# Gate and up of the first layer's experts by seven products of quarters, and a new order of work in the second's

## The chip, the cores and the metric

The kernel runs on one core of a Trainium2 chip. Its time is the device time of one execution in microseconds; lower is better. The engines are TensorE (PE, with its weight loads as PEld), VectorE (DVE), ScalarE (ACT), GpSimd (POOL), and the SyncE queue (SP), which issues most DMAs.

## The reference, cut to what matters

A trunk of two layers over 1024 rows and 256 context rows of 1024 float32 numbers: modulation, a mixer, and then 16 experts. In the first layer the contexts go through the experts too, in the second they don't. What changes lies in the experts:

```python
def expert_choice_ffn(h, w_router, w_gate, w_up, w_down):
    cap = CAPACITY_FACTOR * n // N_EXPERTS            # 128 rows, 32 contexts per expert
    aff = softmax(h @ w_router); gate, idx = top_k(aff.T, cap)
    xg = h[idx]                                       # gathered per expert
    hid = silu(xg @ w_gate) * (xg @ w_up)             # 1024 x 1024 weights for each expert
    out = (hid @ w_down) * gate
    return zeros_like(h).at[idx].add(out)
```

## The kernel before

All matrices are float32; each float32 matmul is two instructions on TensorE. The program is a row of stages (`project`, attention, `mix_out`, `experts`, `front`, `scan`, ...). In a stage each engine has its own instruction stream in program order, tied to the others by semaphores only. Weights for a following stage can be loaded ahead into buffers of classes named `...Ahead` (`FrontAhead` for the stage `front`, `DownAhead` for the first layer's down weights).

**First layer, `experts`** (L2357 on). Per expert, GpSimd gathers 128 rows (`xg`) and 32 contexts (`xc`) by indirect DMA. TensorE transposes them (`turn_rows`, L2711 and L2714), ScalarE and VectorE scale and shift them into `xT` with 160 columns (128 rows, 32 contexts). For each of 8 blocks of 128 hidden columns TensorE multiplies gate and up weights as the standing operand by `xT` (L2756, 8 matmuls each), ScalarE takes silu, VectorE the product; so the hidden values come out already transposed. Down is two halves of 8 matmuls with 512 columns (`down_rows`, L2722), between them the contexts as four strips of 32 output partitions at once (`down_ctx`, L2731). GpSimd adds the results into `moe` by indirect DMA. The stage begins with eight steps each of two thirds of a modulation (`opening`, L244) and ends with eight of another (`closing`). The SP queue's order at the start is: vectors, modulation weights, gate and up of expert 0, the stored first third (`store_third`, which waits until it is in memory), down of expert 0 after the first transposes, `following.load` (some 25 loads, L2313), gate and up of expert 1, the second stored third, 4 MB `load_columns`, down of expert 1, then a loop.

**Second layer, `last_experts`** (L2786 on), no contexts. Gate and up are each made by seven products of quarters in place of eight (the Strassen-Winograd scheme). A quarter product has 4 x 2 matmuls: 64 rows' halves of `xT` (or sums of them, `sx`) stand, 256 columns of weights or of sums of weights stream, and two column halves of the array work at once on the two halves j. VectorE makes the sums of weight quarters (`weight_sum`, four per matrix, 128x2048 numbers each, L3017 to L3026) and of row quarters (`row_sums`). Products share four PSUM banks X, Z, W, V. ScalarE copies four of them out (`keep`), VectorE adds the rest to them (`quarter`) and multiplies (`hidden`). TensorE then transposes the hidden values (`turn_hidden`, L3123), ScalarE copies them to `hT`, and down takes 32 instructions (L3167) into banks W and V, alternating between the two. ScalarE takes the left half of y from W (L2986), VectorE the right half from V. The order of one expert on TensorE:

```python
for i in (GATE, UP):
    for p in PRODUCTS:              # (5, 1, 2, 6, 3, 7, 4)
        multiply(e, i, p)
turn_hidden(e, 0)
turn_rows(e + 1)
turn_hidden(e, 1)
```

Product 2 of gate waits for `ya` (ScalarE has taken the left half of y), product 4 for `yv`. In the last expert the final sums begin: the SP queue first issues `following.load_rows` (8 loads of the rows of `res` into the gate weights' place), then, once the scatter of expert 14 is in memory, the loads of `moe` into `m` (`load_sum`). ScalarE squares them (`square`) between two `keep`, VectorE gates (`gated`, L3063) and sums them (`summed`, L3068).

In `scan`, SP stores eight tiles in order and issues `following.load_qk` for the band attention after the sixth.

## Time and profile before

| | |
|---|---|
| median of 3 runs | 3416.34 us (3415.37 to 3417.86) |
| the profiled execution: time, span | 3414.7 us, 3413.0 us |
| TensorE busy | 3160.0 us, 93% of the span |
| VectorE, ScalarE, GpSimd busy | 46%, 30%, 15% |
| mean granted TensorE clock | 0.962 |
| read from and written to memory | 585.65 MB, 90.97 MB, 198 GB/s |

The profile is of one execution. Busy shares are means over stages with different limits, so each part has to be read in its own window. "Idle before" in square brackets is the time an engine stood before an instruction, with what ended it; times are from the start of the span.

### The profile page before, as it was taken

The numbers are of one execution on the slowest core, as the hardware profiler recorded it, in microseconds if no ns is written. First come the engines' busy times: TensorE is split into PE (matmuls) and PEld (weight loads), VectorE is DVE, ScalarE is ACT, GpSimd is POOL, SyncE is SP. The second block draws the span as 40 slices with busy tenths as digits, with TensorE's granted clock in tenths as the row PEclk, the third lists the DMA queues.
The fourth block names the chain that finished last, engine by engine and source line by source line (L and its number), as shares of the span: only waits on it lengthen the run. The fifth ranks groups of instructions, "written<-read, shape, count | busy, mean of one in ns | idle before, by whom it ended". The sixth has DMA issues, their size and how long they took to land. (4 is left out here: it accounts for less than half of the span.)

```text
span 3413.0 us, 52595 instructions
## 1 busy us (share of the span) xinstructions
PE 3160.0 (93%) x19496; PEld 2216.1 (65%) x19496; DVE 1559.8 (46%) x3170; ACT 1009.8 (30%) x2323; POOL 525.1 (15%) x639
## 2 busy tenths in 40 slices
PE   6999989999987999999999799899899299999996
PEld 4888856667435788787887565666664155555553
DVE  3212178778654010101101254566785666666565
ACT  4111156755330111101111152235554222222222
POOL 0010235110100101011110120254101101111112
PEclk9999999999987999999999899999999599999998
DMA  6336353053639977787777630100414589999996
GB/s 231 130 108 114 92 188 113 20 132 95 241 132 339 352 267 250 244 275 245 265 255 262 232 121 1 56 22 28 112 33 173 197 293 334 326 335 339 338 335 257
DMA packets 340390, 672.38 MB, mean 197 GB/s; under 512 B 84041, under 2 KB 133065, under 8 KB 334017
## 3 DMA queue, kind: packets, MB, share of 16 engines
q1 hardware_dynamic: 308384, 568.00, 47.9%
q0 software_dynamic: 13616, 47.32, 5.5%
q10 hardware_dynamic: 18240, 55.16, 4.3%
q8 instruction: 83, 1.36, 0.2%
q14 instruction: 67, 0.54, 0.1%
HBM read 585.65 MB, written 90.97 MB: 198 GB/s over the span
## 5 line engine op out<-in xcount | busy, mean ns | idle before, releaser
L2756 PE MATMUL experts_gu_ps<-experts_xT,experts_wg 128*128 128x160 f32 x2048 | 301.3, 300 | 2.6 <-DVE experts_xT L2630 2.6
L2756 PE MATMUL experts_gu_ps<-experts_xT,experts_wu 128*128 128x160 f32 x2048 | 299.4, 299 | 0.0
L2756 PEld LDWEIGHTS experts_gu_ps<-experts_xT,experts_wg 128*128 128x128 f32 x2048 | 287.9, 191 | 9.9 <-issue 9.9
L2756 PEld LDWEIGHTS experts_gu_ps<-experts_xT,experts_wu 128*128 128x128 f32 x2048 | 285.6, 190 | 0.0
L2653 DVE TENSOR_TENSOR experts_hid<-experts_sil,experts_gu_ps 128x160 f32<-128x160 f32 x128 | 41.1, 321 | 516.1 <-ACT experts_sil L2584 516.1
L2722 PE MATMUL experts_y_ps<-down_ahead_wd,experts_hid 128*128 128x512 f32 x512 | 228.3, 599 | 0.0
L2584 ACT ACTIVATE experts_sil<-experts_gu_ps 128x160 f32<-128x160 f32 x128 | 38.9, 304 | 604.9 <-PE experts_gu_ps L2756 604.9
L2722 PEld LDWEIGHTS experts_y_ps<-down_ahead_wd,experts_hid 128*128 128x128 f32 x512 | 94.6, 190 | 114.4 <-issue 113.7
L3458 PE MATMUL front_pb_ps<-kept_hT,front_ahead_w 128*128 128x512 f32 (+1 forms) x384 | 138.7, 521 | 0.7 <-DVE kept_dt L3509 0.7
L3167 PE MATMUL experts_w_ps<-experts_wd,experts_hT 128*128 128x512 f32 x256 | 130.8, 597 | 8.5 <-issue 7.8
L3167 PE MATMUL experts_v_ps<-experts_wd,experts_hT 128*128 128x512 f32 x256 | 129.6, 592 | 0.0
L2671 DVE TENSOR_SCALAR experts_y<-experts_y_ps,experts_wt 128x512 f32<-128x512 f32 x16 | 12.0, 751 | 249.0 <-PE experts_y_ps L2722 249.0
L554 PE MATMUL proj_x_ps<-first_w,first_shared 128*128 128x256 f32 x480 | 115.0, 383 | 3.1 <-DMA first_w<-in_l_w_in 3.1
L3912 PE MATMUL scan_f_ps<-scan_w,kept_hT 128*128 128x512 f32 x256 | 116.4, 597 | 0.0
L3458 PEld LDWEIGHTS front_pb_ps<-kept_hT,front_ahead_w 128*128 128x128 f32 x384 | 72.4, 190 | 62.7 <-issue 59.4
L2524 POOL DMA_INDIRECT moe<-experts_yc,experts_ixsc x16 | 25.8, 1610 | 522.5 <-ACT experts_yc L2601 522.5
L2953 ACT ACTIVATE experts_kept<-experts_x_ps 128x256 f32<-128x256 f32 x96 | 36.8, 384 | 231.7 <-PE experts_x_ps L3159 230.4
L554 PEld LDWEIGHTS proj_x_ps<-first_w,first_shared 128*128 128x128 f32 x480 | 91.7, 192 | 15.9 <-DMA first_w<-in_l_w_in 3.4
L635 DVE TENSOR_TENSOR proj_ob<-proj_z_ps,proj_kept 128x256 f32<-128x256 f32 x30 | 12.7, 424 | 190.3 <-PE proj_z_ps L554 189.5
L867 ACT ACTIVATE attn_a_e<-attn_a_e,attn_a_nmx 128x1280 f32<-128x1280 f32 (+1 forms) x80 | 96.6, 1209 | 8.0 <-DVE attn_a_e L929 8.0
L3167 PEld LDWEIGHTS experts_w_ps<-experts_wd,experts_hT 128*128 128x128 f32 x256 | 47.3, 190 | 65.5 <-issue 64.5
L3167 PEld LDWEIGHTS experts_v_ps<-experts_wd,experts_hT 128*128 128x128 f32 x256 | 48.6, 190 | 61.2 <-issue 61.2
(561 smaller groups left out, 6308.7 us busy)
## 6 DMA issues: line engine op xcount, KB each, us to landing
experts_wg<-in_l_w_gate SPq DMA_DIRECT2D x64, 2048.0 KB, 8.5
experts_wu<-in_l_w_up SPq DMA_DIRECT2D x64, 2048.0 KB, 12.7
down_ahead_wd<-in_l_w_down SPq DMA_DIRECT2D x32, 2048.0 KB, 10.6
experts_wd<-in_l_w_down SPq DMA_DIRECT2D x32, 2048.0 KB, 7.7
down_ahead_wd<-in_l_w_mod SPq DMA_DIRECT2D x16, 1024.0 KB, 9.2
proj<-proj_ob ACTq DMA_DIRECT2D x60, 256.0 KB, 2.3
first_w<-in_l_w_in SPq DMA_DIRECT2D x6, 2048.0 KB, 10.1
attn_a_mod_w<-in_l_w_mod ACTq DMA_DIRECT2D x12, 1024.0 KB, 6.5
```

The source lines that it names most:

```text
L554: mm = nc.tensor.matmul(to[:, left], by[k], at[k], start=(k == 0 and n in (0, 1, 5)), stop=(k == HALF - 1 and n in (3, 5, 6)), skip_group_ ...
L635: nc.vector.tensor_tensor(ob[:, slot, 0, right], Z[:, left], kept[:, 2], ALU.add).then_inc(dve_out, 1)
L867: nc.scalar.activation(e[:, s, m, 0:w], e[:, s, m, 0:w], ACT.Exp, bias=nmx[:, s, m:m + 1], scale=-1.0, accum_out=sums[:, s, m:m + 1]).then ...
L2524: pool.indirect_dma_start(moe.rearrange("t (j c) -> (t j) c", j=4), bass.IndirectOffsetOnAxis(ap=ixsc[:, 0:1], axis=0), yc[:], None, compu ...
L2584: nc.scalar.activation(sil[:, f % 2, :], GU[f % 2][:, 0, 0:N], ACT.Silu).then_inc(sil_done, 1)
L2653: nc.vector.tensor_tensor(hid[:, f, :], sil[:, f % 2, :], GU[f % 2][:, 1, 0:N], ALU.mult).then_inc(hid_done, 1)
L2722: mm = nc.tensor.matmul(Y[h][:], hid[:, k, 0:CAPX], wd[:, h, k, :], start=(k == 0), stop=(k == KD - 1))
L2756: mm = nc.tensor.matmul(GU[f % 2][:, part, 0:N], w[:, h, k, c * P:(c + 1) * P], xT[:, k, :], start=(k == 0), stop=(k == KD - 1))
L2953: nc.scalar.activation(kept[:, KEPT.index(p), :], bank[:, 0:COLS], ACT.Copy).then_inc(act_out, 1)
L3167: return nc.tensor.matmul(Y[h][:], hT[:, k, :], w[DOWN][:, k, h * BANK:(h + 1) * BANK], start=(k == 0), stop=(k == KD - 1))
L3458: mm = nc.tensor.matmul(pb[n % 4][:, 0:width], w[:, s, k, at:at + P], hT[:, k, first:first + width], start=(k == 0), stop=(k == KD - 1))
L3912: mm = nc.tensor.matmul(F[:], kept.hT[:, k, t * P:(t + 1) * P], w[:, int(kind == "q"), k, :], start=(k == 0), stop=(k == KD - 1))
```

## The change

`experts` is replaced by `first_experts`, which does gate and up of the 128 rows by the same seven products. Contexts are now gathered as 128 rows of 256 numbers (four strips of one context each) and are multiplied on their own, for gate and for up, in four strips of 32 output partitions (`multiply_ctx`); hidden rows and hidden contexts are transposed afterwards. The sums of weight quarters lie in `following.w`, the weight buffer of `front`, so `load_columns` moves behind the last expert. The gathers run one expert further ahead. In both layers the order of products becomes (5, 1, 2, 4, 6, 3, 7), products 5 and 1 of the next expert's gate go before the down product, the next rows are transposed after product 4 of up, both halves of the gate (and up) weights are loaded after product 7, and the weight sums are made in a new order. In the tail `load_rows` goes behind the first four `load_sum`, and two tiles are gated in advance, not four. In `scan`, `load_qk` goes one store earlier. Three semaphores of `Choice` become one, and two small buffers of the modulation are lent by others.

```diff
-PRODUCTS = (5, 1, 2, 6, 3, 7, 4)
+PRODUCTS = (5, 1, 2, 4, 6, 3, 7)
+def first_experts(nc, name, K, listed, normed, mod, g_pre, w_gate, w_up, w_down, moe, following, down, last_third):
...
+        sums = [following.w[:, i].rearrange("p k n -> p (k n)").rearrange("p (s k j n) -> p s k j n", s=2, k=HALF, j=2) for i in (GATE, UP)]
...
+            def _(sp):
...
+                for n in range(opening.slots, opening.steps):
+                    opening.load(sp, n)
+                for i in (GATE, UP):
+                    for half in range(2):
+                        load(i, half, 0)
+                opening.store_third(sp, 0)
+                sp.wait_ge(opening.multiplied, START + opening.steps)
+                load_down(0)
+                following.load(sp)
+                opening.store_third(sp, 1)
+                with sp.Fori(0, E - 1) as e:
+                    for i in (GATE, UP):
+                        sp.wait_ge(mm_done, multiplied(e, i, 7))
+                        for half in range(2):
+                            load(i, half, e + 1)
+                    sp.wait_ge(y_done, right_at(e))
+                    load_down(e + 1)
+                for i in (GATE, UP):
+                    sp.wait_ge(mm_done, multiplied(E - 1, i, 7))
+                    for n in range(4):
+                        closing.load(sp, 4 * i + n)
+                following.load_columns(sp)
...
+            def _(dve):
...
+                def gates_and_up(e, last=False):
+                    weight_sum(e, UP, 7)
+                    hidden_ctx(e)
+                    after(dve, ht_done, e * 3)
+                    for q in range(4):
+                        quarter(e, GATE, q)
+                    weight_sum(e, UP, 4)
+                    for q in range(4):
+                        if q == 1 and not last:
+                            weight_sum(e + 1, GATE, 5)
+                            ctx_rows(e + 1)
+                        if q >= 2:
+                            dve.wait_ge(hid_done, hidden_at(e, q - 1))
+                        quarter(e, UP, q)
+                        hidden(e, q)
+                        if q == 1 and not last:
+                            row_sums(e + 1, True)
+
+                def rest_of_sums(e):
+                    weight_sum(e, GATE, 6)
+                    row_sums(e, False)
+                    weight_sum(e, GATE, 4)
+                    weight_sum(e, UP, 5)
+                    weight_sum(e, UP, 6)
+                    weight_sum(e, GATE, 7)
...
+                def turn_hidden(e, c):
+
+                    pe.wait_ge(hid_done, hidden_at(e, 2 * c + 2))
+                    pe.wait_ge(hid_out, copied_at(e, 2 * c))
+                    for h in range(2):
+                        for i in range(2):
+                            mm = nc.tensor.transpose(HT[:, 2 * h + i, :], gate[:, c, h, i * P:(i + 1) * P], K.ident[:])
+                    mm.then_inc(ht_done, 1)
...
+                def multiply_ctx(e, i):
+                    if i == GATE:
+                        pe.wait_ge(sx_done, ctx_rows_at(e))
+                        after(pe, hid_done, (e - 1) * 5 + 1)
+                    for half in range(2):
+                        pe.wait_ge(w_in[i][half], START + e * 16 + 16)
+                    for k in range(KD):
+                        for j in range(4):
+                            mm = nc.tensor.matmul(C[j * CAPC:(j + 1) * CAPC, i, :], xcT[:, k, :], w[i][:, k, j * CW:(j + 1) * CW],
+                                                  start=(k == 0), stop=(k == KD - 1))
+                    mm.then_inc(mm_done, 1)
...
+                def from_context_to_rows(e, following_rows):
+                    multiply_ctx(e, UP)
+                    for p in PRODUCTS[2:]:
+                        multiply(e, GATE, p)
+                    turn_hidden_ctx(e)
+                    for p in PRODUCTS:
+                        multiply(e, UP, p)
+                        if p == 4 and following_rows:
+                            turn_rows(e + 1)
+                    if following_rows:
+                        pe.wait_ge(sx_done, ctx_rows_at(e + 1))
+                    turn_hidden(e, 0)
...
+                with pe.Fori(0, E - 1) as e:
+                    from_context_to_rows(e, True)
+                    multiply(e + 1, GATE, PRODUCTS[0])
+                    turn_hidden(e, 1)
+                    multiply(e + 1, GATE, PRODUCTS[1])
+                    multiply_ctx(e + 1, GATE)
+                    pe.wait_ge(xa, START + e * 2 + 4)
+                    down_all(e)
...
 def last_experts(nc, name, K, listed, normed, mod, g_pre, w_gate, w_up, w_down, moe, following, out):
...
-                sp.wait_ge(mm_done, multiplied(E - 1, GATE, 4))
-                following.load_rows(sp, x)
                 sp.wait_ge(s_done, (E - 1) * 16)
...
+                sp.wait_ge(mm_done, multiplied(E - 1, GATE, 7))
+                following.load_rows(sp, x)
...
                 with pe.Fori(0, E - 1) as e:
-                    for i in (GATE, UP):
-                        for p in PRODUCTS:
-                            multiply(e, i, p)
+                    for p in PRODUCTS[2:]:
+                        multiply(e, GATE, p)
+                    for p in PRODUCTS:
+                        multiply(e, UP, p)
+                        if p == 4:
+                            turn_rows(e + 1)
                     turn_hidden(e, 0)
-                    turn_rows(e + 1)
+                    multiply(e + 1, GATE, PRODUCTS[0])
                     turn_hidden(e, 1)
+                    multiply(e + 1, GATE, PRODUCTS[1])
...
-                    if j == NTX - 3:
+                    if j == NTX - 4:
```

## Rows read from the trace of the kernel before

**Rows 1.** Windows, first layer's experts: window, length, busy and count by engine, PEclk, DMA, GB/s.

```profile
1230.00:1500.00 270.00, 270.00 (x1841) 221.10 (x1840) 27.23 (x75) 31.92 (x75) 30.99 (x50) 1.00 0.76 257
```

**Rows 2.** Timeline of TensorE, one expert, first layer: start, length, engine, line, operation.

```profile
1226.20 7.13 PE L2722 MATMUL experts_y_ps<-down_ahead_wd,experts_hid 128*128 128x512 f32 x16
...
1233.17 2.34 PE L2756 MATMUL experts_gu_ps<-experts_xT,experts_wg 128*128 128x160 f32 x16
...
1267.95 1.04 PE L2711 MATMUL experts_tp_ps<-ident,experts_xg 128*128 128x128 f32 x8
...
1269.52 7.13 PE L2722 MATMUL experts_y_ps<-down_ahead_wd,experts_hid 128*128 128x512 f32 x16
...
1276.59 3.66 PE L2731 MATMUL experts_yc_ps<-down_ahead_wd,experts_hid 128*32 128x256 f32 x64
...
1280.18 4.99 PE L2722 MATMUL experts_y_ps<-down_ahead_wd,experts_hid 128*128 128x512 f32 x11
```

**Rows 3.** Timeline of TensorE, one expert, second layer.

```profile
2770.86 1.95 PE L3159 MATMUL experts_z_ps<-experts_tg,experts_sx 128*64 128x256 f32 x16
...
2793.36 1.90 PE L3159 MATMUL experts_v_ps<-experts_tu,experts_xT 128*64 128x256 f32 x16
...
2795.18 0.66 PE L3123 MATMUL experts_ht_ps<-ident,experts_hid 128*128 128x128 f32 x4
...
2796.55 0.60 PE L3123 MATMUL experts_ht_ps<-ident,experts_hid 128*128 128x128 f32 x4
...
2797.67 1.10 PE L3167 MATMUL experts_w_ps<-experts_wd,experts_hT 128*128 128x512 f32 x2 [0.52 <-issue]
...
2811.57 1.95 PE L3159 MATMUL experts_z_ps<-experts_tg,experts_sx 128*64 128x256 f32 x16
```

**Rows 4.** Timeline of ScalarE and VectorE, the same expert of the second layer.

```profile
2793.57 0.38 ACT L2953 ACTIVATE experts_kept<-experts_x_ps 128x256 f32<-128x256 f32 x1 [2.99 <-PE experts_x_ps L3159]
...
2794.45 0.42 DVE L3040 TENSOR_TENSOR experts_hid<-experts_hid,experts_gate 128x256 f32<-128x256 f32 x1
...
2800.63 2.29 DVE L3022 TENSOR_TENSOR experts_wg<-experts_wg 128x2048 f32<-128x2048 f32 x1
...
2811.74 0.69 ACT L2986 ACTIVATE experts_y<-experts_w_ps,experts_wt 128x512 f32<-128x512 f32 x1 [11.09 <-PE experts_v_ps L3167]
```

**Rows 5.** Start of the first layer's experts (timeline); last row: DMA issues, 1150 to 1850.

```profile
1068.69 4.60 PE L2756 MATMUL experts_gu_ps<-experts_xT,experts_wg 128*128 128x160 f32 x16 [2.63 <-DVE experts_xT L2630]
...
1103.06 0.96 SPq L2330 DMA_DIRECT2D front_ahead_cw<-in_l_conv_b  x1
...
1114.23 6.11 SPq L257 DMA_DIRECT2D mod<-experts_opening_rows  x4
...
experts_wg<-in_l_w_gate SPq DMA_DIRECT2D x26, 2048.0 KB, 8.5
```

**Rows 6.** Timeline of the tail: last expert of the second layer and final sums.

```profile
3352.09 0.32 POOL L2920 COPY experts_ixs<-experts_index 128x1 int32<-128x1 int32 x1 [7.79 <-DMA moe<-experts_y,experts_ixs]
...
3353.19 4.91 SPq L2354 DMA_DIRECT2D experts_wg<-res  x8
...
3358.15 23.44 SPq L2884 DMA_DIRECT2D experts_m<-moe  x5
...
3370.40 1.06 ACT L2958 ACTIVATE experts_sq<-experts_m 128x1024 f32<-128x1024 f32 x1 [13.36 <-DMA experts_m<-moe]
...
3373.23 3.68 PE L3159 MATMUL experts_x_ps<-experts_wu,experts_sx 128*64 128x256 f32 x16 [11.45 <-ACT experts_kept L2953]
...
3386.32 1.23 DVE L3063 TENSOR_TENSOR experts_m<-experts_m,finish_ahead_gate 128x1024 f32<-128x1024 f32 x1 [1.49 <-ACT experts_sq L2958]
...
3397.63 1.28 DVE L3068 SCALAR_TENSOR_TENSOR experts_wg<-experts_m,experts_ms,experts_wg 128x1024 f32<-128x1024 f32 x1
```

**Rows 7.** Timeline where the scan stage ends and the band stage begins.

```profile
2396.46 3.71 DVE L3840 SCALAR_TENSOR_TENSOR band_ahead_o<-scan_total,scan_ms,scan_gn 128x256 f32<-128x256 f32 x4
...
2405.38 1.97 PE L1612 MATMUL attn_band_tr_ps<-ident,band_ahead_q 128*128 128x128 f32 x8 [9.56 <-DMA band_ahead_q<-proj]
```

More of the change, by code:

```diff
@@ L2870, in _ @@
                         sp.wait_ge(mm_done, multiplied(e, i, 7))
[L2871 to L2873 removed]
+                        for half in range(2):
+                            load(i, half, e + 1)
                     for half in range(2):
@@ L3985, in trunk @@
                 if with_ctx:
-                    experts(nc, f"experts{n}", K, listed, normed, mods[n], layer["g_pre_ffn"], *weights, moe, following, down, rest[3])
+                    first_experts(nc, f"experts{n}", K, listed, normed, mods[n], layer["g_pre_ffn"], *weights, moe, following, down, rest[3])
                 else:
```

894 lines of the change are left out of this document (464 added, 430 removed).

## The prediction

> **What bounds the kernel now.** I read the page's table of engines first, then the windows of the two expert stages, then TensorE's timeline for one expert of each layer, then what ScalarE, VectorE and the SP queue do beside it, and last the two places where TensorE stands still. In the first layer's experts TensorE is busy for the whole window, at a granted clock of 1.00, while the DMA engines are at 0.76 and VectorE has 27 us of work in 270 [rows 1]. So there the time is TensorE's instruction stream, and nothing else. One expert is 53.98 us from down product to down product: 16 blocks of gate and up (34.78), the transposes of the next rows (1.57), the down products (7.07 and 6.97) and the contexts' down product (3.59) [rows 2]. In the second layer one expert takes 40.71 us: fourteen products of 1.73 (24.23 up to the transposes), transposes of 0.50, 0.87 and 0.50, a stand of about 0.6 until hT is copied, 13.90 for down [rows 3].
>
> **Change part by part, first layer, steady state.** Removed per expert: 34.78 + 1.57 = 36.35. Added: 14 products x 1.73 = 24.2 (the same shape, 16 instructions 128*64 by 256 [rows 3]); the contexts' gate and up as strips, 64 instructions 128*32 by 256 each, the very shape of the contexts' down product, 2 x 3.59 = 7.2 [rows 2]; ten transposes for the next rows (8 rows, 2 contexts) at 0.114 (12 take 1.37 from 2795.18 to 2796.55 [rows 3]) = 1.1; eight of the hidden rows and two of the hidden contexts = 1.2. Sum 33.7.
>
> A new wait: `turn_hidden(e, 1)` needs the last hidden quarter, and product 7 is now the last. After that product's issue ends (2793.36), ScalarE's copy ends 0.6 later, VectorE's sum and product 1.5 later [rows 3, 4]; two more operations of 0.42 make it 2.45, and 0.1 for the semaphore. TensorE arrives at 0.09 + 0.50 + 1.73 = 2.3: a stand of 0.25.
>
> Now VectorE, which had no weight sums there. It gets eight of 2.29 [rows 4], some 18 us, with all else about 28 of 51.6: enough, if nothing it queues behind is late. The gate weights of the next expert are asked for after product 7 of gate. With the end of the previous down product as zero this is 3.6 + 5 x 1.73 + 0.35 = 12.6; 8.5 to landing [rows 5] gives 21.1; the sum for product 5 ends at 23.4, two context operations at 24.3. The up quarter behind them can start at 24.4 anyway, the first hidden transposes come at 25.9, VectorE is ready at 25.3. The margin is 0.6 us. I take 0.2 for both a small lateness and the seams. The up weights (asked at 26.0) are wanted by VectorE from 33.5, where it waits, but TensorE wants them at 51.6; down has 33 us. Gathers run an expert ahead, under all this. The saving is 36.35 - 33.7 - 0.25 - 0.2 = 2.2 per expert, 35 over 16; the last expert also drops the useless transposes (1.1) and waits 0.75 for hT: 0.3 more.
>
> The strips are where a page speaks against this. Row: 64 context instructions take 3.59 us [rows 2], 56 ns each, where a lone 256-column one would take half of the 512-column 0.43 us (16 in 7.07 [rows 2]); four strips thus overlap 3.8 times. The Trainium skill (TensorE: Matmul & The Clock Gate, Measured speedup vs the span model) has 3.07 times for four tiles by rows, and like values for columns. With that the two new context products would cost some 4.5 each, 1.8 more per expert; the row is this very shape, so I go by it.
>
> **First layer, first expert.** This is the largest loss I see. The SP queue issues the loads for the following stage (`following.load`) and the second stored third before its loop; the gate weights of expert 1 come after. Before, the last of `following.load` ends at 1104.02 [rows 5], and expert 0 still ran until about 1122: hidden. Now the stores of the opening third, with their wait for landing, stand ahead of the gate load too. Four took 6.11 with the queue full [rows 5]; with it empty between 2 and 8 with landing, I take 4.5. So the load goes at 1108.5, half lands at 1117.0, sum, context operations, quarter and hidden bring the first hidden transposes to 1121.3. TensorE would be there, starting 0.6 later than at 1068.69 (all eight xT blocks are on ScalarE), with 2.3 for the low clock as in the first block before (4.60 for 2.34 [rows 2, 5]), at 1069.3 + 5.8 + 7.2 + 8.6 + 0.2 + 12.1 + 1.1 = 1104.3. It stands 17.0 us, and then the clock costs another 2.3. Cover: none, VectorE's order puts that sum before the up quarters. Loss 17.0 + 2.3 + 0.6 = 19.9. The 4 MB of columns for the next stage move behind the last expert, since the sums lie in their buffer; they may slow the last scatter by 0 to 2, I take 0.5. First layer: 35.3 - 19.9 - 0.5 = 14.9 gained.
>
> **Second layer.** Products 5 and 1 of the next expert move ahead of down and cover the stand of 0.6 [rows 3]. But product 2 now follows down directly, and it writes the bank W from which ScalarE still takes the left half of y. Both halves end together there, ScalarE starts at 2811.74 and ends at 2812.43 [rows 4]; with 0.15 for the semaphore product 2 starts at 2812.6 and not at 2811.57: 1.0 lost. In the first layer the contexts' up product lies between. Per expert: -0.6 + 0.25 + 1.0 = 0.6 longer, 15 times 9.0. The first expert has all seven sums ahead of its gate quarters: VectorE needs six more of 2.29 and three row sums before the first quarter, 15.9 us, TensorE is there at about 14.8; with the seam 1.3 lost.
>
> The tail. Before, the rows of res (8 loads) go ahead of the sums m; the scatter had landed at 3352.09, m arrives at 3370.40, ScalarE waits for it with `keep` behind it, and TensorE stands 11.45 and then runs a product in 3.68 [rows 6]. Now m goes first, at the scatter's landing, and the stand is gone. What ends last then is the rows: the same bytes, asked for 1 us earlier. m and rows take 18.8 us from 3353.19 by the old rate (17.2 to the ninth load, and three more), so the rows are in 30.6 after the down product of expert 14 (3340.8: 2811.57 [rows 3] and 13 periods; the landing is 11.2 behind it, the first issue 11.8). From there VectorE has eight sums of 1.28 and six gatings of 1.23 [rows 6], 17.6, and 0.5 of waits: 48.7. Before, the last sum ended at 3398.9 [rows 6], 58.1 behind. The gain is 9.4. Second layer: 9.4 - 9.0 - 1.3 = 0.9 lost.
>
> **Scan.** q and k of the band stage are loaded after the fifth stored tile, not the sixth. Two tiles are 3.71 of VectorE, and TensorE waits 9.56 for q [rows 7]: between 0 and 1.9, I take 1.5, as other engines enter the stage about then. Other edits (one semaphore for three in `Choice`, halves of xT) cost nothing: TensorE's stream does not change with them.
>
> **Sum.** 14.9 - 0.9 + 1.5 = 15.5 off the profiled execution's 3414.7 (span 3413.0), 3399.2; the median of the runs is 1.6 above the profiled one. I predict 3400. That is 0.5%; under 0.2% (6.8 us) this kernel can't be told from no change.
>
> **Rivals.**
> 1. *Gate weights late in every expert* (slower). The margin in the first layer is 0.6 us, in the second 0.9. Each us beyond costs 15 or 16. All the gain is eaten when the half lands 10.1 us after its issue, not 8.5. For it: the load now starts as the down weights' 4 MB end, with a scatter and two gathers in flight. The Trainium skill (DMA: Bandwidth & Descriptors, Queues, rings and completion order) says that an engine takes turns between queues packet by packet, so a gather slows the load. Against it: 8.5 was measured with gathers around, and the engines are idle for a quarter of the time [rows 1]. At 2 us late past the margin in both layers the time is 3400 + 16 x 2 + 15 x 2 = 3462, at 1 late in both 3431. Chance 0.11 of more than that 1.5 in all.
> 2. *No stand in the first expert*: the small loads go out faster, or the half lands before 1104. Against: the SP row. Time 3400 - 19 = 3381. Chance 0.08.
> 3. *The wait for W costs less or the tail gives more* (the rows land sooner, TensorE's second layer hides the copy): 3388. Chance 0.14.
> 4. *No measurable change*: the stand is longer (8 us of stores) and the strips or sums lose 0.3 per expert: 3410 to 3422. Chance 0.12.
> 5. *Strips of gate and up overlap worse than those of down*: three at once instead of 3.8, 64 x 0.215 / 3 = 4.6 for 3.59 [rows 2], 2 x 1.0 x 16 = 32 more, 3432. Against: the same shape, measured. Chance 0.01. The page on tiles named above would have it so.
> The forecast itself: 0.54, its own range 3392 to 3408.
>
> Faster by over 0.2%: 0.76, within: 0.12, slower: 0.12. The range, leaving out rivals 5, the far part of 1 and the lower part of 2, is 3380 to 3418.
>
> **What would show it.** Period of the first layer 51.6 to 51.9, and of the second 41.2 to 41.4, with TensorE waiting about 1.0 before `experts_w_ps` for ScalarE's y; one stand of 15 to 19 us before the first `experts_ht_ps` near 1105; a gate load issued near 1108; no wait of ScalarE for m, and VectorE waiting for the rows in the tail. Wrong if the weight sum for product 5 waits for its DMA past 23 us in each expert, or if the strips take more than 3.7.

## The result and the profile after

The changed kernel takes 3440.4 us (median of four runs, 3435.5 to 3442.5) against 3416.7 us for the kernel before, measured beside it. The ratio is 1.0068, 95% interval 1.0054 to 1.0082: slower by 0.7%, where I had forecast 0.5% faster. The profiled execution is the fastest of the four: 3435.5 us, span 3433.7 us, 20.7 more than before.

Three anchors on TensorE split these 20.7 us: the first product of the first layer's experts, the first transposes of `front`, and the transposes of the second layer's `Choice`.

| stretch | before | after | difference | forecast |
|---|---|---|---|---|
| first layer's experts, to `front`'s first transposes | 891.0 | 898.7 | +7.7 | -14.9 |
| `front` and scan, to the second layer's `Choice` | 753.2 | 752.4 | -0.8 | -1.5 |
| from there to the end | 700.1 | 713.9 | +13.8 | +0.9 |
| mean period, first layer / second layer | 53.98 / 40.71 | 53.58 / 41.81 | -0.4 / +1.1 | -2.2 / +0.6 |

One expert of the first layer on TensorE, in the changed kernel's timeline (start, length, engine, line, operation; in brackets the idle time before it and what ended it), against [rows 2]:

```profile
1226.83 0.63 PE L2805 MATMUL experts_ht_ps<-ident,experts_gate 128*128 128x128 f32 x4 [1.08 <-DVE experts_xcT L2669]
1227.38 1.95 PE L2848 MATMUL experts_z_ps<-front_ahead_w,experts_sx 128*64 128x256 f32 x16
1229.26 0.66 PE L2805 MATMUL experts_ht_ps<-ident,experts_gate 128*128 128x128 f32 x4
1229.85 1.95 PE L2848 MATMUL experts_x_ps<-experts_wg,experts_xT 128*64 128x256 f32 x16
1231.73 3.66 PE L2860 MATMUL experts_c_ps<-experts_wg,experts_xcT 128*32 128x256 f32 x64
1235.32 4.99 PE L2868 MATMUL experts_w_ps<-down_ahead_wd,experts_hT 128*128 128x512 f32 x11
...
1275.86 1.90 PE L2848 MATMUL experts_z_ps<-experts_wu,experts_sx 128*64 128x256 f32 x16
1277.58 1.90 PE L2848 MATMUL experts_x_ps<-experts_wu,experts_sx 128*64 128x256 f32 x16
1280.50 0.63 PE L2805 MATMUL experts_ht_ps<-ident,experts_gate 128*128 128x128 f32 x4 [1.02 <-DVE experts_xcT L2669]
```

The strips are as forecast: `experts_c_ps` takes 3.59 (1231.73 to 1235.32). But TensorE stands about 1 us in each expert for VectorE (0.76 to 1.12 in the fourteen experts behind the first, 0.94 in the mean). VectorE's timeline and the SP queue's show why:

```profile
1218.13 0.42 DVE L2716 TENSOR_TENSOR experts_gate<-experts_gate,experts_up 128x256 f32<-128x256 f32 x1
1222.84 2.29 DVE L2690 TENSOR_TENSOR front_ahead_w<-experts_wg 128x2048 f32<-128x2048 f32 x1 [4.29 <-DMA experts_wg<-in_l_w_gate]
1225.05 0.42 DVE L2668 TENSOR_TENSOR experts_xcT<-experts_ht_ps,experts_gain 128x256 f32<-128x256 f32 x1
1225.51 0.43 DVE L2669 TENSOR_TENSOR experts_xcT<-experts_xcT,experts_shift 128x256 f32<-128x256 f32 x1
1225.85 0.42 DVE L2710 TENSOR_TENSOR experts_up<-experts_z_ps,experts_kept 128x256 f32<-128x256 f32 x1
1226.30 0.42 DVE L2716 TENSOR_TENSOR experts_gate<-experts_gate,experts_up 128x256 f32<-128x256 f32 x1
```

```profile
1199.41 1.00 SPq L2507 DMA_DIRECT2D down_ahead_wd<-in_l_w_down  x2
1211.94 0.93 SPq L2501 DMA_DIRECT2D experts_wg<-in_l_w_gate  x2
1225.79 0.92 SPq L2501 DMA_DIRECT2D experts_wu<-in_l_w_up  x2
```

The gate weights are asked for at 1211.94 and the sum for product 5 can start only at 1222.84: 10.9 us, not 8.5. The sum, two context operations, a quarter and a hidden product follow, and then the transposes. The windows of the same expert (length, busy and count of PE, PEld, DVE, ACT, POOL, then clock, DMA share, GB/s):

```profile
1199.30:1211.90 12.60, 12.60 (x147) 7.84 (x146) 4.13 (x5) 0.80 (x3) 5.64 (x6) 1.00 0.90 278
1211.90:1222.80 10.90, 10.90 (x100) 7.24 (x100) 3.90 (x5) 4.23 (x11) 0.67 (x4) 1.00 1.03 402
1222.80:1238.50 15.70, 14.62 (x140) 8.14 (x137) 13.46 (x16) 3.76 (x12) 0.00 (x0) 1.00 0.97 373
1238.50:1253.00 14.50, 14.50 (x90) 6.38 (x88) 4.49 (x2) 2.65 (x4) 1.62 (x1) 1.00 0.08 10
```

The mean DMA share over this expert (some 0.7) hides two halves: 39 us with the engines full, 14.5 us with nothing to move. The gate load falls into the full part.

The first expert, at the place of [rows 5] (TensorE, then SP):

```profile
1102.61 1.90 PE L2848 MATMUL experts_x_ps<-experts_wu,experts_sx 128*64 128x256 f32 x16
1117.65 1.08 PE L2805 MATMUL experts_ht_ps<-ident,experts_gate 128*128 128x128 f32 x4 [13.14 <-DVE experts_xcT L2669]
1118.66 3.16 PE L2848 MATMUL experts_z_ps<-front_ahead_w,experts_sx 128*64 128x256 f32 x16
1121.76 0.66 PE L2805 MATMUL experts_ht_ps<-ident,experts_gate 128*128 128x128 f32 x4
```

```profile
1101.92 0.59 SPq L2330 DMA_DIRECT2D front_ahead_cw<-in_l_conv_b  x1
1102.55 1.33 SPq L257 DMA_DIRECT2D mod<-experts_y  x4
1105.39 1.03 SPq L2501 DMA_DIRECT2D experts_wg<-in_l_w_gate  x2
```

The stand is there, for the reason given, at 13.1 instead of 17.0: the stores took 2.8 us with their wait, not 4.5, and the small loads ended 1.5 earlier. Behind this stand the granted clock is 0.50 (1.2 GHz) in the transposes and 0.59 in product 5: the two take 4.1 us from start to start (1117.65 to 1121.76), where they take 2.4 two experts later (1226.83 to 1229.26).

Second layer, against [rows 3]: the stand for y is there too, and the period is 41.81 (2825.02 to 2866.83).

```profile
2825.02 1.95 PE L3313 MATMUL experts_w_ps<-experts_wg,experts_xT 128*64 128x256 f32 x16 [0.84 <-ACT experts_y L3134]
...
2866.83 1.95 PE L3313 MATMUL experts_w_ps<-experts_wg,experts_xT 128*64 128x256 f32 x16 [0.84 <-ACT experts_y L3134]
```

The tail, against [rows 6]: SP asks for `m` first, ScalarE waits only 1.2 us for it, and VectorE then waits for the rows of `res`.

```profile
3379.40 1.77 SPq L3019 DMA_DIRECT2D experts_m<-moe  x4
3381.21 5.31 SPq L2354 DMA_DIRECT2D experts_wg<-res  x8
```

```profile
3400.97 2.48 DVE L3225 SCALAR_TENSOR_TENSOR experts_wg<-experts_m,experts_ms,experts_wg 128x1024 f32<-128x1024 f32 x2 [9.14 <-DMA experts_wg<-res]
```

The seam between scan and the band stage, against [rows 7]: first VectorE's last tile before the change, then SP, VectorE and TensorE in the changed kernel.

```profile
2402.41 0.88 DVE L3840 SCALAR_TENSOR_TENSOR band_ahead_o<-scan_total,scan_ms,scan_gn 128x256 f32<-128x256 f32 x2 [0.76 <-DMA mixed<-band_ahead_o]
```

```profile
2403.85 1.11 SPq L1194 DMA_DIRECT2D band_ahead_q<-proj  x2
2406.12 7.19 SPq L3841 DMA_DIRECT2D mixed<-band_ahead_o  x3
```

```profile
2412.08 0.88 DVE L4001 SCALAR_TENSOR_TENSOR band_ahead_o<-scan_total,scan_ms,scan_gn 128x256 f32<-128x256 f32 x2 [5.38 <-DMA mixed<-band_ahead_o]
```

```profile
2413.76 1.94 PE L1612 MATMUL attn_band_tr_ps<-ident,band_ahead_q 128*128 128x128 f32 x8 [12.88 <-PEq L3817]
```

The sixth tile's store now stands behind the loads of q and k, and VectorE waits 5.38 us for its buffer before the last tile, not 0.76. TensorE no longer waits for q but for the end of the stage, and longer: 12.88 us, not 9.56.

### The profile page after: what moved, and what is told of

It reads as the page before. It is cut to its first block and busy times, and to the rows that moved or that the text cites. A ratio compares the mean times of both kernels' runs of the same rounds, so it can differ in the third digit from the quotient of the medians.

```text
span 3433.7 us, 57319 instructions
## 1 busy us (share of the span) xinstructions
PE 3144.1 (92%) x21080; PEld 1975.6 (58%) x21080; DVE 1888.4 (55%) x3373; ACT 1086.4 (32%) x2510; POOL 554.7 (16%) x641
## 5 line engine op out<-in xcount | busy, mean ns | idle before, releaser
L2868 PE MATMUL experts_w_ps<-down_ahead_wd,experts_hT 128*128 128x512 f32 x256 | 114.1, 599 | 0.7 <-ACT experts_hT L2633 0.7
L2868 PE MATMUL experts_v_ps<-down_ahead_wd,experts_hT 128*128 128x512 f32 x256 | 114.1, 599 | 0.0
L2606 ACT ACTIVATE experts_kept<-experts_x_ps 128x256 f32<-128x256 f32 x96 | 36.8, 383 | 202.5 <-PE experts_x_ps L2848 202.5
L3054 POOL DMA_INDIRECT moe<-experts_y,experts_ixs x15 | 24.1, 1609 | 464.0 <-DVE experts_y L3240 464.0
L3091 ACT ACTIVATE experts_kept<-experts_x_ps 128x256 f32<-128x256 f32 x96 | 36.8, 383 | 179.8 <-PE experts_x_ps L3313 176.8
L929 DVE TENSOR_SCALAR_CACHE_REDUCE attn_a_e<-attn_a_s_ps,attn_a_nmx 128x256 f32<-128x256 f32 (+1 forms) x128 | 72.8, 613 | 27.3 <-PE attn_a_s_ps L1004 27.2
L1029 PE MATMUL attn_a_o_ps<-attn_a_v,attn_a_aT 128*128 128x128 f32 x672 | 83.1, 277 | 3.9 <-ACT attn_a_sq L882 3.9
L2777 DVE TENSOR_SCALAR experts_y<-experts_v_ps,experts_wt 128x512 f32<-128x512 f32 x15 | 11.3, 752 | 137.0 <-PE experts_v_ps L2868 137.0
L2598 ACT ACTIVATE experts_xT<-experts_tp_ps,experts_shift,experts_gain 128x128 f32<-128x128 f32 x128 | 47.9, 459 | 120.6 <-PE experts_ht_ps L2796 120.6
L1029 PEld LDWEIGHTS attn_a_o_ps<-attn_a_v,attn_a_aT 128*128 128x128 f32 x672 | 78.3, 192 | 11.4 <-issue 7.7
L3083 ACT ACTIVATE experts_xT<-experts_tp_ps,experts_shift,experts_gain 128x128 f32<-128x128 f32 x128 | 47.9, 460 | 110.0 <-PE experts_tp_ps L3268 110.0
```

The costliest lines, as they stand in the source:

```text
L929: nc.vector.tensor_scalar(e[:, s, m, c:c + w], S[i % 2][m][:, 0:w], -1.0, nmx[:, s, m:m + 1] if j else None, ALU.mult, ALU.min, accum_out= ...
L1029: mm = nc.tensor.matmul(O[:, 0:P], aT[:, kt, :], v[:, h % 2, kt, :], start=(kt * P == keys(t)[0]), stop=(kt == last))
L2598: a = nc.scalar.activation(xT[:, k, :], TP[k // 4][:, k % 4, :], ACT.Identity, bias=shift[:, 0, k:k + 1], scale=gain[:, 0, k:k + 1])
L2606: nc.scalar.activation(kept[:, KEPT.index(p), :], bank[:, 0:COLS], ACT.Copy).then_inc(act_out, 1)
L2868: mm = nc.tensor.matmul(Y[h][:], hT[:, k, :], wd[:, h, k, :], start=(k == 0), stop=(k == KD - 1))
L3083: a = nc.scalar.activation(xT[:, k, :], TP[k // 4][:, k % 4, :], ACT.Identity, bias=shift[:, k:k + 1], scale=gain[:, k:k + 1])
```

## The experiments

All ratios are to the kernel before, measured beside each kernel, with intervals of 0.0010 to 0.0014 to each side. "First layer" and "rest" are the first and third stretch of the table above, read in each kernel's one trace; a period stands for one expert near 1280 or 2900. Stretches with the same code differ by up to 2.3 us from trace to trace (first layer of the changed kernel and of e4: 898.7 and 896.4), so a difference of 2 us between two rows says nothing.

| kernel | ratio | first layer | period | rest | period |
|---|---|---|---|---|---|
| before | 1 | 891.0 | 53.98 | 700.1 | 40.71 |
| changed | 1.0068 | 898.7 | 53.7 | 713.9 | 41.81 |
| e1_columns_later | 1.0052 | 893.3 | 53.4 | 713.9 | |
| e2_sum_later | 1.0090 | 905.8 | 54.06 | 713.6 | |
| e3_stagger | 1.0060 | 898.5 | 53.55 | 713.9 | |
| e4_six_first | 1.0024 | 896.4 | | 701.3 | 40.91 |
| e5_ctx_first | 1.0027 | 886.4 | 52.64 | 714.8 | |
| e6_gather_early | 1.0041 | 886.8 | 52.61 | 714.5 | |
| e7_down_early | 1.0032 | 886.5 | 52.61 | 713.4 | |
| e8_mended | 0.9940 | 871.9 | 52.61 | 696.8 | 40.91 |
| e9_also_gather | 0.9930 | 872.1 | | 696.1 | 40.91 |
| e10_joined | 0.9926 | 871.9 | | 692.9 | 40.71 |
| e11_split_rows | 0.9950 | 871.5 | | 701.3 | 41.21 |
| e12_old_second | 0.9945 | 872.1 | | 698.5 | 40.71 |

**e1_columns_later.** The first gate and up loads of expert 1 go ahead of the stores and of `following.load`.

```diff
                 load_down(0)
+                for i in (GATE, UP):
+                    sp.wait_ge(mm_done, multiplied(0, i, 7))
+                    for half in range(2):
+                        load(i, half, 1)
+                    if i == GATE:
+                        opening.store_third(sp, 1)
                 following.load(sp)
-                opening.store_third(sp, 1)
-                with sp.Fori(0, E - 1) as e:
+                sp.wait_ge(y_done, right_at(0))
+                load_down(1)
+                with sp.Fori(1, E - 1) as e:
```

> The changed kernel, with one thing moved: in the first layer the SP queue issues the first gate and up loads of expert 1 ahead of the opening third's stores and of the 26 small loads for the next stage. Theory (the SP queue held the gate load back in the first expert alone): the gate load goes at 1090 to 1092 instead of 1105.4, the stand of 13.1 us before the first hidden transposes goes with it, and with it the low clock behind it (1.4 to 2.3): 14 to 16 us less than the changed kernel, ratio to the kernel before about 1.002, periods unchanged at 53.7 and 41.8. Rival (the small loads only move and hold back the down or up loads of expert 1, or the weights land late anyway as 6 MB are then in flight): a stand of 5 us or more stays in the first two experts, less than 8 us gained.

The first stand went: the first down product starts at 1111.7 instead of 1127.8. But the small loads now kept the SP queue until 1140.6, past the end of expert 0, and the down and gate loads of the next expert came at 1140.7 and 1142.5. A second stand takes half of it back:

```profile
1153.97 1.90 PE L2855 MATMUL experts_x_ps<-experts_wu,experts_sx 128*64 128x256 f32 x16
1163.63 1.08 PE L2812 MATMUL experts_ht_ps<-ident,experts_gate 128*128 128x128 f32 x4 [7.76 <-DVE experts_xcT L2676]
```

The first layer is 5.4 us shorter, not 15. The theory names the right queue; the rival is right that the wait only moves, with 36 us of small loads in one piece. This run also has the gate load right behind the down weights (1.8 us): VectorE starts the sum at 1159.65, 17.2 us after the issue.

**e2_sum_later.** VectorE's sum for product 5 goes behind the up quarter, its hidden product and the row sums.

```diff
                         if q == 1 and not last:
-                            weight_sum(e + 1, GATE, 5)
                             ctx_rows(e + 1)
...
                         if q == 1 and not last:
                             row_sums(e + 1, True)
+                            weight_sum(e + 1, GATE, 5)
```

> The changed kernel, with VectorE's weight sum for product 5 of the next expert put behind the second up quarter, its hidden product and the row sums in the first layer; nothing else. Theory (TensorE stands 1.1 us in each expert because the two context operations, the quarter and the hidden product are queued behind a sum that waits for a half of the gate weights): the stand before the hidden transposes goes, what may be left before product 5 is 0 to 0.4 us; period 52.6 to 52.9 instead of 53.7, 12 to 16 us less in all, and the first expert's stand moves behind the hidden transposes and is 2 us shorter. Rival (the landing is so late that product 5 waits in place of the transposes): the stand is the same 1 us, now before experts_z_ps, period 53.5 or more, less than 4 us gained.

A miss: 7 us slower in the first layer. TensorE no longer waits before the transposes, but before product 5:

```profile
1275.94 0.66 PE L2805 MATMUL experts_ht_ps<-ident,experts_gate 128*128 128x128 f32 x4
1277.97 1.95 PE L2848 MATMUL experts_z_ps<-front_ahead_w,experts_sx 128*64 128x256 f32 x16 [1.37 <-DVE front_ahead_w L2690]
```

It isn't the landing that it waits for, as the rival had it. VectorE's timeline has the sum start at 1275.56 without a wait, behind a quarter that needs up product 3, the sixth in order (issued until 1274.1), its hidden product and the row sum. The sum was late by its place in the queue. So 2.29 us of sum fit neither behind that quarter nor, with a landing 10.9 us after the issue, quite in front of it.

**e3_stagger.** The second half of the gate weights is asked for later.

```diff
                         sp.wait_ge(mm_done, multiplied(e, i, 7))
-                        for half in range(2):
-                            load(i, half, e + 1)
+                        load(i, 0, e + 1)
+                        if i == GATE:
+                            sp.wait_ge(mm_done, multiplied(e, UP, 1))
+                        load(i, 1, e + 1)
```

> The changed kernel, with the second half of the gate weights asked for after the first layer's up product 1 instead of together with the first half (3.5 us later). Theory (two halves issued together share the engines, so the first one lands 10.8 us after its issue instead of the 8.5 that I took): the first half lands some 2 us sooner, the stand of 1.1 us per expert goes, the second half lands no later than now; 12 to 16 us less in all, period 52.6 to 52.9. Rival (the first half is slow because of the down weights, gathers and scatters ahead of it, not because of its twin): the sum still starts 10 us or more behind the issue, period 53.5 or more.

The rival holds: asked for at 1267.23 and alone, the first half still lets the sum start only at 1277.95, 10.7 us later. So sharing its first 3.5 us with the twin is not what slows it.

**e4_six_first.** In the second layer product 6, which needs neither W nor V, follows down.

```diff
+    ORDERS = ((5, 1, 6, 2, 4, 3, 7), PRODUCTS)
...
-            return START + e * 14 + (7 * i + PRODUCTS.index(p) + 1)
+            return START + e * 14 + (7 * i + ORDERS[i].index(p) + 1)
...
-                    for p in PRODUCTS[2:]:
+                    for p in ORDERS[GATE][2:]:
                         multiply(e, GATE, p)
```

> The changed kernel, with the second layer's gate products in the order 5, 1, down of the expert before, 6, 2, 4, 3, 7 instead of 2, 4, 6, 3, 7. Product 6 adds to bank X, which no output lies in. Theory (TensorE stands 0.95 us per expert for ScalarE's y in bank W): the stand goes, period 40.8 to 41.0 instead of 41.8, 13 to 16 us less in all. What is then left over 40.71, the period before, is the price of more changes between products and transposes. Rival (product 2 or 4 then waits for something else, such as VectorE's half of y, or the sum for product 6 is late): period 41.5 or more, less than 5 us gained.

Period 40.91, 12.6 us less behind `Choice`, ratio down by 0.0044. The wait for y in bank W was worth what the rows had said.

**e5_ctx_first.** Context operations ahead of the sum.

```diff
                         if q == 1 and not last:
-                            weight_sum(e + 1, GATE, 5)
                             ctx_rows(e + 1)
+                            weight_sum(e + 1, GATE, 5)
```

> The changed kernel, with the two context operations of the next expert ahead of the weight sum for product 5 on VectorE in the first layer (they need only the transposed context rows, which are there 3 us before the gate weights). The run with the sum behind the row sums showed that its queue place is bound from both sides: there the sum waited for the third up product, here it keeps its place before it. Theory (what makes TensorE stand is the chain landing, sum 2.3, then everything queued behind): 0.8 us of the chain go, the stand before the hidden transposes is 0.2 to 0.4 instead of 1.1, period 52.9 to 53.0, 11 us less than the changed kernel. Rival (the landing moves later with the faster period, since the down and gate loads are a fixed amount of traffic per expert): stand 0.6 or more, 5 us or less gained.

Period 52.64, first layer 12.3 us shorter. The landing stayed at 10.6 us after the issue (1264.92 to 1275.52), so 0.8 us less work behind it was nearly the whole stand.

**e6_gather_early.** Gathers when the left half of down is done, not behind the scatter.

```diff
                     chosen(e)
-                    scatter(e)
+                    pool.wait_ge(y_done, left_at(e))
                     gather(e + 2)
+                    scatter(e)
```

> The changed kernel, with the first layer's gathers for the expert after next issued when the left half of down is done, ahead of the scatter, and no longer right behind the scatter. Theory (the gate weights land 10.8 us and not 8.5 us after their issue because scatter, gathers and 4 MB of down weights stand ahead of them in the same 24 us, and the gathers are 0.6 MB of it): the down weights land 1.5 to 2 us sooner than 14.1, the gate half 1 to 2 us sooner, the stand of 1.1 us is gone, period 52.6 to 52.9, 12 to 16 us less than the changed kernel. Rival (the gathers are small beside 6 MB; what counts is down weights alone): down weights land less than 1 us sooner, stand 0.6 or more.

**e7_down_early.** The left half of the down weights when the contexts' down product is done.

```diff
+                    sp.wait_ge(y_done, ctx_at(e))
+                    load_down(e + 1, (0,))
                     sp.wait_ge(y_done, right_at(e))
-                    load_down(e + 1)
+                    load_down(e + 1, (1,))
```

> The changed kernel, with the left half of the first layer's down weights asked for when the contexts' down product is done (7 us sooner, in a stretch where the engines move 10 GB/s), the right half as before. Theory (the gate weights queue behind what is left of the down weights): 2 MB of the 4 leave the stretch ahead of the gate loads, the gate half lands 8 to 9 us after its issue, as in the kernel before, VectorE no longer holds TensorE, period 52.6 to 52.9, 12 to 16 us less. Rival (the gate half is slow by itself, whatever is ahead of it): landing 10.5 us or more as in the run with the second half held back, period 53.5 or more.

Each of the two alone removes the stand. In the first of them the gate load is issued at 1263.54, in the second at 1265.14, and VectorE starts the sum 8.7 and 8.0 us later. The sum in e6, then in e7:

```profile
1272.24 2.29 DVE L2691 TENSOR_TENSOR front_ahead_w<-experts_wg 128x2048 f32<-128x2048 f32 x1 [2.08 <-DMA experts_wg<-in_l_w_gate]
```

```profile
1273.12 2.29 DVE L2692 TENSOR_TENSOR front_ahead_w<-experts_wg 128x2048 f32<-128x2048 f32 x1 [1.37 <-DMA experts_wg<-in_l_w_gate]
```

Medians from issue to landing, 1280 to 1800, of the changed kernel, of e6 and of e7:

```profile
down_ahead_wd<-in_l_w_down SPq DMA_DIRECT2D x20, 2048.0 KB, 14.1
...
experts_wg<-in_l_w_gate SPq DMA_DIRECT2D x18, 2048.0 KB, 13.0
```

```profile
down_ahead_wd<-in_l_w_down SPq DMA_DIRECT2D x20, 2048.0 KB, 13.3
experts_wg<-in_l_w_gate SPq DMA_DIRECT2D x20, 2048.0 KB, 11.3
```

```profile
down_ahead_wd<-in_l_w_down SPq DMA_DIRECT2D x20, 2048.0 KB, 9.6
experts_wg<-in_l_w_gate SPq DMA_DIRECT2D x20, 2048.0 KB, 10.2
```

So what makes the gate half late is the traffic ahead of it, and 0.6 MB less of it is enough. In e6 the down weights land only 0.8 us sooner, less than I had expected and as its rival had it, but the stand is gone all the same. The Trainium skill (DMA: Bandwidth & Descriptors, Queues, rings and completion order) has an engine alternate between queues packet by packet; e6 agrees with it: with the gathers moved away, the SP queue's gate half lands 8.7 us after its issue, not 10.9.

**e8_mended.** All of it together, with the small loads cut in two (behind the up loads issued in experts 1 and 2, counted from 0), and two semaphores for the rows in the tail.

```diff
                 load_down(0)
-                following.load(sp)
-                opening.store_third(sp, 1)
-                with sp.Fori(0, E - 1) as e:
+                for e in range(3):
+                    for i in (GATE, UP):
+                        sp.wait_ge(mm_done, multiplied(e, i, 7))
+                        for half in range(2):
+                            load(i, half, e + 1)
+                        if i == GATE and e == 0:
+                            opening.store_third(sp, 1)
+                    if e == 1:
+                        following.load(sp)
+                    if e == 2:
+                        following.load_rest(sp)
...
-                dve.wait_ge(following.x_in, START + 16 * NTX)
                 for t in range(NTX):
+                    if t % 4 == 0:
+                        dve.wait_ge(following.x_in[t // 4], START + 64)
```

> The changed kernel with the causes found so far mended together: the first gate and up loads of expert 1 ahead of the opening third's stores, and the small loads for the next stage cut in two, behind the up loads of experts 1 and 2 (in one piece behind those of expert 0 they held the down and gate loads of expert 1 back, a second stand of 7.8 us); the left down half early; the context operations ahead of the sum; product 6 first behind down in the second layer; and in the tail a semaphore for rows 0 to 3 of res and one for rows 4 to 7, so that VectorE starts when the first four are in. Theory: no stand over 0.5 us in the first layer, 15 us for the first expert, 15 for its period (52.6 to 52.8), 15 in the second layer (period 40.9), 3 to 6 in the tail: 3388 to 3394, ratio 0.993 to 0.995. Rival (stands only move, as in the run with the small loads later): over 3405.

3394.6 us (3389.5 to 3396.9), ratio 0.9940. No stand is left between the first product and the last expert of the first layer; it is 26.7 us shorter than in the changed kernel. From the last down product to the end it takes 37.1 us instead of 40.4: VectorE waits 5.5 us for rows, not 9.1.

**e9_also_gather.** Both e6 and e7 in the mended kernel.

> The mended kernel with the early gathers as well. Each of the two, left down half early and gathers early, had brought the first layer's period alone to 52.61 us with no stand. Theory (TensorE's stream is the only bound left there, so more room for the gate weights is worth nothing): period 52.6, ratio within 0.1% of the mended kernel's. Rival (the transfers still cost something that shows as no stand): 3 us or more less.

Nothing more in the first layer (872.1 against 871.9), as expected of a stretch with no stand. The ratios differ by 0.0010, inside their intervals.

**e10_joined and e11_split_rows.** In the second layer of the mended kernel, one group of transposes fewer, or one more, with the same instructions.

```diff
-                    turn_hidden(e, 0)
                     multiply(e + 1, GATE, PRODUCTS[0])
-                    turn_hidden(e, 1)
+                    for c in range(2):
+                        turn_hidden(e, c)
                     multiply(e + 1, GATE, PRODUCTS[1])
```

> The mended kernel, second layer: the two groups of four hidden transposes in one place, behind the next expert's product 5, so that TensorE changes from products to transposes and back once less per expert. Theory (the 0.8 to 1.3 us per expert of the first layer, and most of what the second layer has over its sum, which no stand explains, is 0.2 to 0.3 at each such change and back): period 40.6 to 40.7 instead of 40.91, 3 to 4 us less over 15. Rivals: the changes cost nothing and the blocks are longer for another reason, 40.9; or the copies of hT now come late (2.3 us behind the transposes, with one product of 1.73 as cover) and put a stand of 0.3 to 0.6 before down, 41.0 or more.

```diff
-                        if p == 4:
-                            turn_rows(e + 1)
+                        if p in (2, 4):
+                            turn_rows(e + 1, (p // 4,))
```

> The mended kernel, second layer: the eight transposes of the next rows cut in two groups of four, behind up products 2 and 4, so that TensorE changes to transposes and back once more per expert; the same instructions otherwise. Theory (0.2 to 0.3 at each change and back): period 41.1 to 41.2 instead of 40.91, 3 to 4 us more over 15. Rival (a change costs nothing): 40.9.

Periods 40.71 and 41.21 against 40.91, with no stand in any: 0.2 less and 0.3 more. Two groups of four transposes with a product between, in e11:

```profile
2890.90 1.90 PE L3334 MATMUL experts_w_ps<-experts_wu,experts_xT 128*64 128x256 f32 x16
2892.73 0.66 PE L3288 MATMUL experts_tp_ps<-ident,experts_xg 128*128 128x128 f32 x4
2893.31 1.95 PE L3334 MATMUL experts_v_ps<-experts_tu,experts_xT 128*64 128x256 f32 x16
2895.19 0.66 PE L3288 MATMUL experts_tp_ps<-ident,experts_xg 128*128 128x128 f32 x4
2895.78 1.95 PE L3334 MATMUL experts_x_ps<-experts_tu,experts_sx 128*64 128x256 f32 x16
2897.55 1.90 PE L3334 MATMUL experts_z_ps<-experts_wu,experts_sx 128*64 128x256 f32 x16
```

A product among products takes 1.73 from start to start. `experts_w_ps` here takes 1.83 until the transposes start, `experts_v_ps` between two groups 1.88, `experts_x_ps` behind one 1.77, and four transposes 0.58 where eight take 1.02. e10 has the lowest median of the case: 3390.6 us (3387.3 to 3393.0), ratio 0.9926, interval 0.9912 to 0.9939, which overlaps those of e8 and e9.

**e12_old_second.** The mended first layer with the second layer as it was before.

> The mended kernel's first layer, with the second layer's experts as they were before the change, tail included. Theory (all of what the mended kernel gains, 22 us of span, comes from the first layer, by period 52.61 against 53.98 and the moved start, and 0.7 from the scan; the second layer's change is worth nothing in its period, and its tail 2 to 3 us): 3393 to 3396, ratio 0.994 to 0.9955, second layer's period 40.71. Rival (the second layer's change carries part of the gain): over 3400.

3396.4 us, ratio 0.9945. The first layer alone carries nearly all of the gain. The second layer's change, mended, can't be told from none (696.8 against 698.5, while the kernel before, with the second layer of e12, reads 700.1). Joined it reads 5.6 less. Its period is then the old one, 40.71; from the end of expert 14's down product to the end of the kernel it takes 60.9 us against 70.6, and from its first product to the end of the first expert's down product 47.2 against 42.5. So what it gains, it gains in the tail.

## Why the prediction was wrong

It fell on the slower side: 3440, where I had 3400 and a range to 3418. Step by step:

**The gate half's landing (failed; first layer).** "8.5 to landing gives 21.1 ... The margin is 0.6 us." The issue came where I had it, 12.6 after the down product (1211.94). The landing did not: 8.5 was measured where gate weights were asked for 17.5 us behind the down weights, as the SP queue of the kernel before shows:

```profile
1287.34 1.00 SPq L2439 DMA_DIRECT2D down_ahead_wd<-in_l_w_down  x2
1304.88 0.38 SPq L2432 DMA_DIRECT2D experts_wg<-in_l_w_gate  x1
```

Here they are asked for 12.5 us behind, with a scatter and, new in this change, two gathers in the same stretch. e3 rules out the twin half in the first 3.5 us, e6 and e7 show that traffic ahead of it does it, e5 that the work queued behind the sum turns it into a stand: 0.94 us in the mean of fourteen experts. The landing was 2.4 late against a margin of 0.6, so 1.8 should have stood; it was less because TensorE came 0.5 later than I had it (the passages below) and VectorE's work behind the landing took 4.0, not 4.2. This was my rival 1, at 0.11. I had the mechanism, and argued it away with the mean DMA share of [rows 1], which says nothing of the 39 us in which the load falls: in the last microseconds ahead of the gate load's issue the share was 0.57 before the change (1302 to 1305, issue at 1304.88) and is 1.03 here (1263 to 1265, issue at 1265.67).

**"0.2 for both a small lateness and the seams" (failed; both layers).** With every stand gone the first layer's period is 52.61 (e6 to e8), where my sum of instructions is 33.7 - 36.35 + 53.98 = 51.3. What is over, 1.3, is the change of shape between blocks. I priced blocks by rows from the middle of long runs. The old expert passes from one kind of block to another five times (gate and up, transposes, down, contexts, down), the new one 14 times, and e10 and e11 give 0.10 and 0.15 for one passage (two fewer, 0.2; two more, 0.3): nine more are 0.9 to 1.4. Only the second layer was varied, but the first layer's own timeline has the 1.3 as block lengths (e6, 1224.66 to 1277.28, no stand): the fourteen products take 24.9 where I had 24.2, each of those beside transposes 1.77 to 1.88; the twenty transposes take 2.8 where I had 2.3, priced in a run of twelve; the contexts' strips 7.2, as forecast; down 17.7, 0.1 over. In the second layer the mended period, 40.91, is the old one less its stand of 0.52 [rows 3] plus 0.7, for five more passages (eight instead of three): the same price.

Together: per expert I had a saving of 2.2. Lateness took 0.94 and passages 1.3, less the 0.45 that I had set aside for a wait and seams: 0.4 is left. The wait of 0.25 before `turn_hidden(e, 1)` was wrong too; there is none in either layer, with or without the stand before.

**First expert (right, too large).** Place and cause as forecast. 13.1 for 17.0, 1.7 for the low clock (4.1 for 2.4) instead of 2.3. The 0.6 was not there (the first product starts at 1068.74, before at 1068.69), and the 0.5 for the last scatter can't be told (TensorE's stand before `front` is 18.09, before 17.69, and 17.55 to 18.02 in the experiments). The sum for the first layer: 13.1 + 1.7 lost, 5.4 given back by the fourteen periods between the first and the fifteenth down product; the rest, 1.7, is what is left over in the first and last expert. That makes +7.7, where 35.3 was to be given back.

**Second layer (right mechanism, too small).** The stand of 1.0 for y in W is there (0.84 in the rows, 1.0 from the last down block) and e4 takes it away. The period is 1.1 longer and not 0.6, by passages again. A slip without effect: the fourteen products take 24.32 from 2770.86 to 2795.18 [rows 3], not 24.23.

**Tail (one sum wrong, one too large).** Measured from the end of expert 14's down product (3367.6) the rows are in after 33.4 us instead of 30.6, and the end comes 6.1 us sooner than before instead of 9.4. And I left something out: that point now has products 5 and 1 of the last expert ahead of it, 3.6 us, which the first expert's 1.3 should have held. The right sum by my own numbers was 14 x 0.6 + 1.3 + 3.6 - 9.4 = 3.9 lost, not 0.9; measured were 13.8: 14 x 1.1, 4.5 for the first expert, 6.1 back.

**Scan (failed, and hidden in the stretch).** "Between 0 and 1.9, I take 1.5": the step that failed is the overlap, for it took no account of the stores that the load now stands ahead of. From VectorE's first row of [rows 7] (in the changed kernel at 2401.52) to the first band product it takes 12.2 us instead of 8.9, 3.3 more, by the wait for the sixth store; TensorE's stand there is 12.3 to 13.4 in all thirteen kernels with this code (the changed one and the twelve experiments). From the band stage's first product to `Choice` 1.4 comes back (306.1 for 307.5), for a reason that was not looked for. The whole stretch is 0.8 less in the trace, but from 752.1 to 757.0 in those thirteen, so the net can't be told, and no run undid the edit.

**Strips, rival 5.** 3.59, as the row said. The Trainium skill (TensorE: Matmul & The Clock Gate, Measured speedup vs the span model) has 3.07 times for four tiles by rows; here four tiles by columns are 3.8 times as fast as one, and for them the measurement decides. The formula in the same section, the length of one and 4 ns more for each further tile, gives 3.8 too: an estimate by it, from 215 ns for one.

## What to carry to other kernels

A duration from issue to landing belongs to the traffic in which it was measured: when a load moves, look at what was issued in the 15 us ahead of it in the new order, and at the DMA share of that window, not of the stage. Where a stream is cut into more and smaller blocks of different shapes, count the passages between shapes and price them from a place where two shapes meet. When a list of small loads holds a queue, moving it shifts the wait unless the gap it moves into is as long as the list; cut it to the gaps. When a load moves up in a queue, ask what it now stands ahead of, and who waits for that.

## What was unexpected

In a period of 53.7 us the DMA engines moved 402 GB/s over 11 us and 10 GB/s over 14.5 us. Moving 2 MB, or 0.6 MB of gathers, out of the full part was worth 12 us over the kernel, though the kernel's total traffic stayed the same (673 MB). And a passage between products and transposes costs TensorE 0.10 to 0.15 us although it never stands in the trace: the time sits in block lengths (1.83 and 1.88 for 1.73).

A load moved ahead of stores, to have it sooner, put off what it was meant to bring forward: q was asked for earlier, the store behind it held VectorE for 4.6 us more, and the band stage's first product came 3.3 us later.
